# Two experts per slot for the 64 (head, sample) rows of a one-core decoder step: 128-row gathers, four turns per layer in place of eight

## What is computed

```python
q = (xb @ w_q).reshape(PEER_BLOCK, PEER_HEADS, 2, PEER_HALF)
s = jnp.einsum('thpc,hpnc->thpn', q, subkeys)
vals, idx = lax.top_k(s, PEER_TOPK)              # 16 of 128 keys, on two sides
...                                              # best 16 of the 16 x 16 sums
e = (i1 * PEER_N_KEYS + i2)                      # experts: 8 heads x 16 per token
g = jax.nn.softmax(best, axis=-1)
a = gelu(einsum('td,tkd->tk', xb, u[e]))
y = einsum('tk,tkd->td', g * a, v[e])
```

## Times and profile before

| | us |
|---|---|
| median of the runs shown (3595.45 to 3605.79) | 3595.87 |
| the profiled execution | 3592.32 |
| its span, first to last instruction | 3590.5 |

### The profile page before, as it was taken

How to read it: one execution, slowest core, us unless ns; L and a number is a source line. 1 busy time by engine, 2 the same in 40 slices (tenths; PEclk the granted TensorE clock), 3 DMA queues, 4 the chain that set the end, 5 groups by cost and what they waited for, 6 DMA issues and landing times.

```text
span 3590.5 us, 40191 instructions
## 1 busy us (share of the span) xinstructions
PE 2848.8 (79%) x11531; PEld 1264.3 (35%) x11531; DVE 2295.5 (64%) x6409; ACT 1049.6 (29%) x4473; POOL 1224.3 (34%) x1093
## 2 busy tenths in 40 slices
PE   4888987978889958989989779889865765676757
PEld 0345563434444423434433234334321331122311
DVE  1454457887777856777777567777766445555463
ACT  0212223433434412433434224434311111111111
POOL 0000003433333423434434334434434344434442
PEclk7988998989999978989999989999977777667775
DMA  9750019999999999999999999999999999989996
GB/s 338 253 195 35 1 66 394 400 365 418 371 378 419 393 356 364 414 403 407 412 391 409 394 373 418 415 409 416 387 414 413 410 420 412 319 304 419 421 421 164
DMA packets 202135, 1266.46 MB, mean 353 GB/s; under 512 B 24017, under 2 KB 45058, under 8 KB 62129
## 3 DMA queue, kind: packets, MB, share of 16 engines
q0 software_dynamic: 151040, 1091.03, 75.7%
q1 hardware_dynamic: 50873, 172.85, 12.6%
HBM read 1260.46 MB, written 3.79 MB: 352 GB/s over the span
## 4 chain that ended last, share of the span: by engine, by line
PE 42%; DMA 28%; DVE 15%; issue 7%; ACT 4%; POOL 2%; SPq 1%; DVEq 0%; POOLq 0%; ACTq 0%; PEldq 0%
PE bank L1089 17%; DMA ring<-in_uv,work 10%; DMA mod_mix<-in_uv,work 7%; DMA big<-in_uv,work 6%; PE bank L829 6%; PE bank L941 5%; DVE ring L1906 2%; DMA ring<-in_w_ada 2%; PE bank L846 2%; PE bank L650 2%; PE bank L774 2%; ACT work L1393 1%; DMA work<-in_cache_mla 1%; PE bank L609 1%; PE bank L679 1%
## 5 line engine op out<-in xcount | busy, mean ns | idle before, releaser
L1089 PE MATMUL bank<-ring,work 128*64 128x512 f32 (+1 forms) x2112 | 944.5, 718 | 275.3 <-ACT work L1393 275.1
L1433 POOL DMA_INDIRECT ring<-in_uv,work x528 | 603.3, 1143 | 967.0 <-PE bank L1089 853.3
L1906 DVE CUSTOM_DVE_ANT_0 ring<-ring,mod_smp 128x1024 f32<-128x1024 f32 x512 | 621.7, 1224 | 265.3 <-DMA ring<-in_uv,work 258.0
L1433 POOL DMA_INDIRECT big<-in_uv,work x264 | 312.3, 1183 | 726.2 <-PE bank L1089 364.3
L1380 ACT ACTIVATE work<-work 128x2 f32<-128x2 f32 (+1 forms) x528 | 106.8, 202 | 1508.3 <-DVE work L1906 1507.9
L829 PE MATMUL bank<-big 128*128 128x512 f32 x1024 | 509.4, 620 | 0.0
L1089 PEld LDWEIGHTS bank<-ring,work 128*64 128x64 f32 (+1 forms) x2112 | 216.4, 154 | 658.8 <-ACT work L1393 390.2
L1089 PE MATMUL bank<-big,work 128*64 128x512 f32 (+1 forms) x1056 | 325.6, 720 | 154.2 <-ACT work L1393 154.0
L1906 DVE CUSTOM_DVE_ANT_0 big<-big,mod_smp 128x1024 f32<-128x1024 f32 x256 | 309.6, 1224 | 139.4 <-DMA big<-in_uv,work 135.6
L1089 PE MATMUL bank<-work 128*64 128x512 f32 (+1 forms) x528 | 308.2, 712 | 102.1 <-ACT work L1393 101.9
L1393 ACT ACTIVATE work<-small,work 128x64 f32<-128x64 f32 (+1 forms) x1056 | 308.6, 339 | 184.7 <-DVE work L1917 139.0
(11 more groups left out here) (280 smaller groups left out, 3492.1 us busy)
## 6 DMA issues: line engine op xcount, KB each, us to landing
big<-in_wk SPq DMA_DIRECT2D x48, 1152.0 KB, 9.8
ring<-in_w_ada SPq DMA_DIRECT2D x64, 768.0 KB
work<-in_cache_mla SPq DMA_DIRECT2D x104, 160.0 KB, 9.1
ring<-in_uv,work POOLq DMA_INDIRECT x528, 11.5
big<-in_uv,work POOLq DMA_INDIRECT x264, 12.1
ring<-in_w_mla_out SPq DMA_DIRECT2D x1, 4096.0 KB, 12.9
big<-ada_rows SPq DMA_DIRECT2D x8, 512.0 KB, 14.8
big<-in_w_mla_out SPq DMA_DIRECT2D x4, 1024.0 KB, 11.5
```

The lines of the kernel that those rows point to most:

```text
L1089: last = mm(out, diag[0:rows, t % 2, j, 0:min(m, HALF)], s[0:rows, D + half * 512:D + (half + 1) * 512], start=(k == 0 and (n < S0 or j == ...
L1433: pool.indirect_dma_start(slot[g % SLOTS][0:m, :], None, T["uv"].rearrange("l e d -> (l e) d"), bass.IndirectOffsetOnAxis(index[0:m, k * G ...
L1906: dve.tensor_tensor_reduce(u, u, hb[0:m, :], 1.0, 0.0, ALU.mult, ALU.add, dots[0:m, at:at + 1]).then_inc(sem("dots_set"), 1)
```

## The change

A sample slot holds two experts for each of the 64 (head, sample) rows: partitions 0 to 63 the first, 64 to 127 the second. So a sample stage has 8 gathers of 128 rows in place of 16 of 64, and four turns in place of eight. `opens[7]`, and all that is hung on it, comes four turns earlier, and the program has 520 turns. The hidden state is repeated over 128 partitions, DVE, ACT and PE work on 128 partitions in a sample turn, and the samples' choice now goes through `chosen`, `spread_choice` and `place_choice` as that of a prompt tile does (two matmuls in place of four), with the wait of POOL on `expert_set`. The core of the diff:

```diff
-        expert_s = region(work, TOPK, W).bitcast(U32)
-        gate_s = region(work, TOPK, W)
+        expert_s = region(work, TOPK // 2, W).bitcast(U32)
+        gate_s = region(work, TOPK // 2, W)
...
-        TILE_TURNS, SMP_TURNS = KK // GRP, TOPK // GRP
+        TILE_TURNS, SMP_TURNS = KK // GRP, TOPK // GRP // 2
...
                 for half in range(2):
-                    last = mm(pb[2 + half][0:SROWS, :], sel[0:NS, :], hid_s[0:NS, half * 512:(half + 1) * 512], start=True, stop=True)
+                    for e in range(2):
+                        last = mm(pb[2 + half][e * SROWS:(e + 1) * SROWS, :], sel[0:NS, :], hid_s[0:NS, half * 512:(half + 1) * 512],
+                                  start=True, stop=True)
...
-                for g in range(2):
+                for g in range(2 if n < S0 else 1):
                     for e in range(2):
                         last = mm(pb[1][e * HALF:(e + 1) * HALF, g * TOPK:(g + 1) * TOPK].rearrange("p (k s) -> p k s", k=2),
-                                  ident[:, g * HALF:(g + 1) * HALF], chosen[:, n % 2, :, e * 8:(e + 1) * 8], start=True, stop=True)
+                                  ident[0:ranked_rows(n), g * HALF:(g + 1) * HALF], chosen[0:ranked_rows(n), n % 2, :, e * 8:(e + 1) * 8], start=True, stop=True)
...
-                if t - 1 in ranks and ranks[t - 1][2] == 3 and ranks[t - 1][0] < S0:
+                if t - 1 in ranks and ranks[t - 1][2] == 3:
                     spread_choice(*ranks[t - 1][0:2])
...
-                        last = mm(out, diag[0:rows, t % 2, j, 0:min(m, HALF)], s[0:rows, D + half * 512:D + (half + 1) * 512],
+                        last = mm(out, diag[:, t % 2, j, 0:min(m, HALF)], s[:, D + half * 512:D + (half + 1) * 512],
...
-                    if n < S0:
-                        pool.wait_ge(sem("expert_set"), rank_no(n, k // (TOPK // GRP)) + 1)
-                    else:
-                        pool.wait_ge(sem("choice_set"), rank_no(n, 0) + 1)
+                    pool.wait_ge(sem("expert_set"), rank_no(n, k // (TOPK // GRP)) + 1)
...
-                    pool.indirect_dma_start(slot[g % SLOTS][0:m, :], None, T["uv"].rearrange("l e d -> (l e) d"),
-                                            bass.IndirectOffsetOnAxis(index[0:m, k * GRP + j:k * GRP + j + 1], 0))\
+                    pool.indirect_dma_start(slot[g % SLOTS], None, T["uv"].rearrange("l e d -> (l e) d"),
+                                            bass.IndirectOffsetOnAxis(index[:, k * GRP + j:k * GRP + j + 1], 0))\
...
                 dve.wait_ge(sem("choice_ps"), no + 1)
+                if n >= S0:
+                    ts(expert_s, pb[1][:, 0:TOPK // 2], 1.0, None, ALU.mult)
+                    ts(gate_s, pb[1][:, TOPK // 2:TOPK], 1.0, None, ALU.mult).then_inc(sem("expert_set"), 1)
+                    dve.wait_ge(sem("expert_set"), no + 1)
+                    return
```

More of the change, by code:

```diff
@@ L280, in decoder_step @@
         ADA_PLAN = (0, 2, 2, 2, 3, 3, 3, 3, 3, 3, 3, 3, 3, 3, 3, 3, 4, 4, 4)
-        rows_of = lambda n: P if n < S0 else SROWS
+        ranked_rows = lambda n: P if n < S0 else SROWS
         outs_of = lambda n: P if n < S0 else NS
@@ L976, in sample_scores @@
                 if h == 0:
-                    pe.wait_ge(sem("expert_set"), S0 * PH)
+                    pe.wait_ge(sem("expert_set"), rank_no(n, 0))
                 for side in range(2):
@@ L1080, in expert_turn @@
                 last_k = (TILE_TURNS if n < S0 else SMP_TURNS) - 1
-                m, rows = outs_of(n), rows_of(n)
+                m = outs_of(n)
                 if k == 0 and i:
@@ L1319, in copy_repeated @@
                 for half in range(2):
-                    last = act.activation(hid_8[0:SROWS, half * 512:(half + 1) * 512], pb[2 + half][0:SROWS, :], ACT.Copy)
+                    last = act.activation(hid_8[:, half * 512:(half + 1) * 512], pb[2 + half][:, :], ACT.Copy)
                 last.then_inc(sem("rep_ready"), 1)
             def soften_best(n, h):
-                m = rows_of(n)
+                m = ranked_rows(n)
                 best, soft_n = best2[n % 2], soft_n2[n % 2]
@@ L1377, in gelu_turn @@
             def gelu_turn(t):
-                m = rows_of(at_turn[t][1])
                 act.wait_ge(sem("dots_set"), (t + 1) * GRP)
-                act.activation(acts[0:m, t % 2 * GRP:(t % 2 + 1) * GRP], dots[0:m, t % 2 * GRP:(t % 2 + 1) * GRP], ACT.Gelu)\
+                act.activation(acts[:, t % 2 * GRP:(t % 2 + 1) * GRP], dots[:, t % 2 * GRP:(t % 2 + 1) * GRP], ACT.Gelu)\
                     .then_inc(sem("acts_set"), 1)
@@ L1384, in scale_turn @@
                 n = at_turn[t][1]
-                m, o = rows_of(n), outs_of(n)
-                scale_rows = fold if n < S0 else selT[0:SROWS, :]
-                o = min(o, HALF)
+                scale_rows = fold if n < S0 else selT
+                o = min(outs_of(n), HALF)
                 act.wait_ge(sem("wts_set"), t + 1)
@@ L1392, in scale_turn @@
                     at = t % 2 * GRP + j
-                    act.activation(diag[0:m, t % 2, j, 0:o], scale_rows, ACT.Copy, scale=wts[0:m, at:at + 1]).then_inc(sem("diag_set"), 1)
+                    act.activation(diag[:, t % 2, j, 0:o], scale_rows, ACT.Copy, scale=wts[:, at:at + 1]).then_inc(sem("diag_set"), 1)
             for t in range(FIRST, TURNS):
@@ L1696, in rank @@
             def rank(n, h, part, between):
-                l, m, no = layer_of(n), rows_of(n), rank_no(n, h)
+                l, m, no = layer_of(n), ranked_rows(n), rank_no(n, h)
                 a = n % 2 if n < S0 else 0
@@ L1782, in rank @@
                     e(ts(e_side[0:m, 0:TOPK], e_side[0:m, 0:TOPK], float(NK), float(l * NK * NK), ALU.mult, ALU.add))
-                    e_dst, g_dst = (chosen[:, n % 2, 0, :], chosen[:, n % 2, 1, :]) if n < S0 else (expert_s[0:m, :], gate_s[0:m, :])
+                    e_dst, g_dst = chosen[0:m, n % 2, 0, :], chosen[0:m, n % 2, 1, :]
                     need(first + 6)
@@ L1902, in expert_dots @@
                     dve.wait_ge(sem(f"uv_in{g % SLOTS}"), 16 * (g // SLOTS + 1))
-                    u = slot[g % SLOTS][0:m, 0:D]
+                    u = slot[g % SLOTS][:, 0:D]
                     at = t % 2 * GRP + j
                     hb = hid_rep[:, j, :] if n < S0 else hid_8
-                    dve.tensor_tensor_reduce(u, u, hb[0:m, :], 1.0, 0.0, ALU.mult, ALU.add, dots[0:m, at:at + 1]).then_inc(sem("dots_set"), 1)
+                    dve.tensor_tensor_reduce(u, u, hb, 1.0, 0.0, ALU.mult, ALU.add, dots[:, at:at + 1]).then_inc(sem("dots_set"), 1)
             def expert_weights(t):
                 i, n, k = at_turn[t]
-                m = rows_of(n)
                 g_all = gate[n % NT] if n < S0 else gate_s
@@ L1916, in expert_weights @@
                 cols = slice(t % 2 * GRP, (t % 2 + 1) * GRP)
-                tt(wts[0:m, cols], acts[0:m, cols], g_all[0:m, k * GRP:(k + 1) * GRP], ALU.mult).then_inc(sem("wts_set"), 1)
+                tt(wts[:, cols], acts[:, cols], g_all[:, k * GRP:(k + 1) * GRP], ALU.mult).then_inc(sem("wts_set"), 1)
             for t in range(FIRST, TURNS):
```

## The result

The changed kernel's median is 3520.16 us (3519.22 to 3524.87), the kernel before had 3595.66 (3592.74 to 3605.79): ratio 0.9786, interval [0.9772, 0.9800]. The forecast was 3515.2 us. The profiled execution took 3520.84 us with a span of 3519.0, against 3590.5 before, so its span fell by 71.5 us where 80.7 were forecast.

The account below looks back on a forecast made before the run. Prompt turns were taken as bound by gathers, sample stages by PE. Savings of 8.2 (entries), 39.0 (S1) and 33.5 us (S0), with 0 for additions and tile 7, gave 3595.9 - 80.7 = 3515.2 us; range 3504 to 3536.

Parts of the forecast that it names:

- What bounded the kernel: Prompt turns are bound by gathers, sample stages S0 and S1 by PE, in unbroken blocks of 41.1 and 54.8 us.
- Part 1, the entries: Entry to each sample stage: full gathers let the last prompt slot land on time, 4.1 us per stage, 8.2 us together.
- rival that the late slot has another cause: At the stage entries: full gathers save nothing and both stages start 4.1 us later; 3523.4 us, chance 0.07.
- the one by which the samples' rows are slow to fetch: Sample gathers: low rate belongs to the rows, a full gather takes 5.2 us; some 33 us saved, 3563 us, chance 0.04.
- Part 2, the clock: Sample stages: with 128-row matmuls PE's clock reaches its upper level 4.1 us into the stage; records then 0.43 us each.
- rival of the low clock: Sample stages: PE's clock stays low, 27.4 us per stage; 3532.9 us, at worst 3541.0, chance 0.20.
- Part 2, S1: Last sample stage: four turns with 32 records take 15.8 us in place of 54.8, saving 39.0 us.
- Part 2, S0: First sample stage: 19.6 us including two spreadings, in place of 53.1, saving 33.5 us.
- Part 3, nothing for the additions: Prompt turns of tiles 6 and 7: added records, copies and waits are covered by gathers, cost 0, at most 3.5 us per layer.
- the slower rival: Turns `opens[6]` + 38 and `opens[7]` + 50: the new wait outweighs the gain from a 60.2 us hold per layer; chance 0.01.
- Part 4, tile 7: Tile 7 after S0: begins with the same fill and keeps its 348 us; change 0, with 5 us either way.
- the limit of 353 us for the tile: Tile 7: growth beyond 353 us would show the forecast wrong.

Follow-up runs that it names:

- the first experiment: Kernel before with sample gathers filling 128 partitions (64 rows twice), still eight turns and 64-row sample matmuls: 3587.77 us, ratio 0.9975.
- experiments 1 and 2: Kernel before with full 128-partition sample gathers in eight turns; sample matmuls of 64 rows, then of 128: 3587.77 us and 3560.54 us.
- the second experiment: Kernel before with full 128-partition sample gathers, still eight turns, but sample matmuls of 128 rows (second copy gated 0): 3560.54 us, ratio 0.9896.
- the chain shifted: Changed kernel with tile 7's background chain that prepares S1 (norm to ranking) six turns later: 3518.83 us, ratio 0.9782 against the kernel before.
- the spaced version: Changed kernel with the S1-preparing chain's three holds in turns 3, 8, 12 instead of 3, 5, 7: 3511.18 us, again 3510.40 us.

## Why the prediction came out

**What bounded the kernel: right.** PE's two blocks were the bound, and nearly all of the gain came from them: 71.1 of the 71.5 us in the two sample stages, with 8.7 more at the entries and 8.5 lost elsewhere.

**Part 1, the entries: right.** 4.6 and 4.1 us for 4.1 each. The full gathers alone gave 9 to 10.7 us in the first experiment, with an interval from 4.3 to 13.3. The rival that the late slot has another cause falls, and so does the one by which the samples' rows are slow to fetch (it expected 5.2 us for a full gather and 200 GB/s; in S1 the first two sample dots start 2.48 us apart and the rate is 420 to 423 GB/s). One reservation: with full gathers but not both stages packed, S1's last prompt slot came 3.42 us after the one before in three profiles, 0.94 late; in the changed kernel it was on time.

**Part 2, the clock: right.** With S1's first matmul at 3496.79 and 0.88 in the stretch 3500 to 3504, the upper level was there for 0.76 x 4 = 3.04 us, so from 3501.0, 4.2 us into the stage; in S0 the clock was 0.74 in 3120 to 3124, which gives 4.3. The forecast had 4.1 from the earlier trace rows. That the level rises with 128 rows and not with 64 is shown by the pair of experiments 1 and 2, which differ in nothing else. That the moment agrees to 0.2 us is luck. In the second experiment's S1 the clock was 0.64 in 3520 to 3524, so it rose 2.6 us after the first matmul at 3520.29, and with the chain shifted it rose 5.9 us into S0 (0.71 in 3120 to 3124, first matmul at 3116.41); over the 18 stages with 128 rows that were profiled, the first turn took between 4.87 and 6.51 us. The forecast's own row also counts from 78.47, while PE's work had begun at 77.17 with the eight small records of line 628; counted from there it gives 5.4 us. The Trainium skill, TensorE: Matmul & The Clock Gate, Part 1, names sustained matmul activity alone: by that the first experiment should have left the low level, and for 54.9 us of it without a pause it did not. The rival of the low clock, to which I gave 0.20, is out: S1 took 17.1 us, not 27.4.

**Part 2, S1: mechanism right, size 1.2 us too good.** The forecast was 15.8 us to the end of the last matmul; it took 17.0, and 17.1 to `routed`. The last turn waited for the last slot, as forecast. The term that was off is the pace of the sample gathers. From the second sample dot (3491.91) to the eighth (3507.90) are 15.99 us, where six gathers at 2.48 are 14.9. The sixth slot, at 3502.73, came 3.38 us after the one before, 0.9 late, and the seventh 0.3 more, while the DMA engines kept moving 421 GB/s. So something else was moved, and SP's timeline has it: as soon as `routed` is done, SP copies tile 7's finished rows, 0.52 MB, to the output `y_p`.

```profile
3495.96 0.34 SPq L380 DMA_DIRECT2D out_y_p<-x_tok  x1
```

At 422 GB/s those bytes are 1.2 us, the size of the miss; that is an estimate, and no run left the copy out. Before the change the copy stood in the same place (3529.68) and fell under PE's 54.8 us. In the two repeats of the changed kernel the sixth slot came 4.36 and 4.53 us after the fifth, and the stage took 18.0 and 18.1 us, so there S1 was 2.1 to 2.2 us too good, and about one of them has no explanation here.

**Part 2, S0: right** (33.3 for 33.5; PE worked 19.1 us in it, forecast 19.6).

**Part 3, nothing for the additions: not contradicted.** Upstream of S0, where half of them lie, 1.5 us were lost. Between profiles of the same kernel this differs by more: tile 6's third-last dot starts at 3102.98, 3102.79 and 3107.56 us in the three profiles of the changed kernel. So the cost is bounded at a few us, and not shown. The hold of over 60 us that the slower rival needed did not come.

**Part 4, tile 7: the step that failed.** It was written that tile 7 "begins with the same fill". It doesn't. The last two of its first eight slots are issued at the same point relative to the stage's end, which was all that the prediction looked at. But S0 is 33 us shorter and its gathers follow one another almost without a gap, so, as the rows read, these two queue behind gathers that haven't landed yet, and land some 3 us later. That is 2.7 to 3.5 us at the 7th dot, and 3.0 to 7.4 at the 127th; past the first slots the loss seems to need the chain for S1 in tile 7's first turns. Of the 7.0 us in the profiled pair, some 3 are the excess of that one profile over its two repeats. By the first profile the loss is outside the 5 us that were allowed for, by the repeats (345.5 and 345.2 against 341.9, 3.6 and 3.3 us) inside, and the limit of 353 us for the tile held: from its first matmul to `routed`, as the forecast counted it, the tile took 351.2 us (3141.82 to 3493.06), against 348.4 before.

Of the 9.2 us by which the saving fell short, tile 7 is 7.0, the stretch upstream 1.5 and S1 1.2, and 0.5 came back at the entry to S0 (7.0 + 1.5 + 1.2 - 0.5 = 9.2). That sum holds for this one pair of profiles. By medians the saving fell short of 80.7 by 5.2 us here, and by 1.0 and 0.3 us in the two later groups, where chance alone is worth several us. My theory that a later place cures tile 7 held up to its 65th dot and fell for the total: what shifting gained, the ranking, shifted with it, lost again. What helped was distance between the holds, and whether that repairs the loss of the tight S0 or another, older one stays open, since the spaced version was not run with a loose S0.

## What to carry to other kernels

When a stage is split between engines, look at the entry row by row: a half-width gather can cost the full-width ones ahead of it their pace, so filling all partitions pays twice, once in the entry and once in the number of matmuls. When a stage in front of another is shortened, don't take the next one's fill as given; count what is still in flight when it starts. Holds that follow one another closely empty a ring of fixed depth, and the same holds spaced so that the ring refills between them cost less, while moving all of them together gained in one place and lost as much in another. And when a stage that was bound by an engine becomes bound by transfers, look for plain copies in it that had been hidden: they now take their turn among the gathers.

## What the runs showed of the hardware

- Rows of the matmul and the clock: 64 rows by 8 columns of weights, 512 moving columns, fp32, kept PE busy without a pause for 54.9 us at 0.50; with 128 rows and all else equal the clock was at 1.00 from the stretch 3524 to 3528 on. In the four stages with 128 rows read here the rise came 2.6 to 5.9 us after the first matmul.
- A gather of 64 partitions occupied the DMA engines as long as one of 128: twice the bytes made the kernel 0.0025 [0.0012, 0.0037] faster. The Trainium skill, SBUF — State Buffer, Door 1: The DMA port swizzle, gives half the ports to partitions 0 to 63, and the rates here (180 and 211 GB/s against 420 to 424) agree.
- Gathers that overlap in the queue share the engines with a plain copy issued while they are under way: at an unchanged 421 to 423 GB/s one slot came 3.38 us after the one before, the next after 2.74, and the one after that after 2.43, and the copy's 0.52 MB are about what the gathers lost (an estimate from the rate, not tried by a run).
